# A two-block network in one kernel: VectorE makes the low weights of the up product from the ninth step on

## The chip, the core and the metric

The kernel runs on one core of one Trainium2 chip. The metric is device time in microseconds, the median of several executions. Engines: TensorE (PE; its weight loads are shown apart as PEld), VectorE (DVE), ScalarE (ACT), GpSimd (POOL) and SyncE (SP), which here issues nearly all transfers.

## What is computed

The reference is two blocks on 1024 tokens of width 1024 in float32, each with a feed-forward:

```
h = h + jnp.square(jax.nn.relu(m @ w_up[i])) @ w_down[i]         # first block,  m  = rmsnorm(h, norm_mlp[i])
x = x + jnp.square(jax.nn.relu(h2 @ w_up[l])) @ w_down[l]        # second block, h2 = rms_norm(x, norm_mlp_g[l])
```

with `w_up` 1024 x 4096 and `w_down` 4096 x 1024. Ahead of them stand attention and a gated delta rule (first block), or a pooling mixer and a gated recurrence (second block); the change leaves those alone but for the name of a semaphore at the start.

## The kernel before

**Split products.** A float32 product is made on TensorE from operands in a shorter format: each operand is a high part (rounded) plus a low part (value less high part), and high x high, high x low and low x high are added up. So every block of weights needs a high copy `w_hi`, made by ScalarE (`part_hi`, line 1735), and a low one `w_lo`, here made by GpSimd (`mlp`, lines 699 to 708) as four subtractions of 128 columns.

**The feed-forward** (`mlp` in each engine's program) uses a seven-product scheme for 2 x 2 blocks. The up product takes the 16 pairs of column blocks: pair 0 as two ordinary products, pairs 1 to 15 in seven steps each, 105 steps. The down product has four quarters `c` of seven products `q` with four column blocks `m`, 112 steps. A step is 12 matmuls of 128x512: eight with `w_hi` against the operand's high and low part, then, after a wait for `part_lo`, four with `w_lo`. Steps 105, the first of the down product, and 213 have the operand's low part last instead. The four slots of `w_hi` and `w_lo` rotate, so ScalarE makes the high weights of step g+4 when step g is over (`step_done`), GpSimd the low ones after that (`part_hi`), and `part_lo` counts the steps whose low weights are there.

**VectorE** makes the sums of weight blocks that are the sources of steps (`up_sum`, four per pair, into `w_raw` and `w_sum`), adds the products from PSUM into `tmp` (`up_step`), takes ReLU and scale (`relu_r`), forms the operand sums of the down product (`h_sums`, `h_last_sum`), and at the start the sums for operands 7, 5, 6 and 4 (`t_sums`, `t_lo`). In the down product it adds products (`down_step`), makes weight sums (`down_sums`, `down_sum4`), the low parts of the operands (`h_lo`) and, in the last quarter, the shared adds (`shared_adds`). Each engine works its list in order; a wait holds everything behind it.

**SyncE** loads blocks of `w_up` (`load_up`, line 544), stores operand sums to `h_ops` (`store`, line 560) and loads them back with `w_down` (lines 547, 557), also in the order written.

## Time and profile before

| | us |
|---|---|
| median of 3 runs | 2366.03 (2365.56 to 2367.23) |
| profiled execution | 2365.18 |
| its span, first to last instruction | 2363.4 |

| engine | busy us | share of the span | instructions |
|---|---|---|---|
| TensorE | 2339.2 | 99% | 15442 |
| VectorE | 1730.1 | 73% | 2319 |
| GpSimd | 1690.3 | 72% | 2442 |
| ScalarE | 924.0 | 39% | 1478 |

The granted TensorE clock is 0.998 of full speed over the span. The first feed-forward's 217 steps run from 553 to about 1147 us, the second's from 1753 to about 2350 us. Busy time of TensorE counts a matmul from its start to its modelled end, and matmuls overlap, so 99% does not say that none was late: that is read from the distance of their starts, or from how many of them a stretch holds.

### The profile page before, as it was taken

How to read it: one execution, taken by the hardware profiler on the slowest of the kernel's cores; microseconds unless marked ns; L12 is line 12 of the kernel's file. 1: busy time of each engine (PE TensorE's matmuls, PEld its weight loads, DVE VectorE, ACT ScalarE, POOL GpSimd, SP SyncE). 2: the span in 40 equal slices, each digit the busy share in tenths (PEclk: the TensorE clock that was granted, in tenths of full speed). 3: DMA queues.
4: the chain of work that ended last, by engine and by line, in shares of the span. 5: the costliest groups of instructions: out<-in, count | busy, mean ns of one | idle time of the engine just before them, and what ended most of it. 6: DMA issues, size and time to landing. Idle time of an engine off the chain costs nothing.

```text
span 2363.4 us, 40498 instructions
## 1 busy us (share of the span) xinstructions
PE 2339.2 (99%) x15442; PEld 1872.8 (79%) x15442; DVE 1730.1 (73%) x2319; ACT 924.0 (39%) x1478; POOL 1690.3 (72%) x2442
## 2 busy tenths in 40 slices
PE   9999999999999999999999999999999999999998
PEld 7767777777888888888788888888878888888886
DVE  4585656549777787789656777778388777888877
ACT  3152323225333343444424444444163333344443
POOL 5623444457988888988677766557669988898886
PEclk9999999999999999999999999999999999999999
DMA  5200000312444475443022111113114444654342
GB/s 173 72 19 29 29 28 28 117 36 89 166 153 150 147 252 194 170 152 116 19 80 92 46 37 37 37 44 119 47 48 174 156 148 147 241 194 150 125 144 106
DMA packets 110871, 254.55 MB, mean 108 GB/s; under 512 B 9440, under 2 KB 9952, under 8 KB 108512
## 3 DMA queue, kind: packets, MB, share of 16 engines
q1 hardware_dynamic: 105264, 233.43, 28.5%
q10 hardware_dynamic: 5424, 18.62, 2.3%
q8 instruction: 123, 2.02, 0.3%
q14 instruction: 60, 0.49, 0.1%
HBM read 181.75 MB, written 67.63 MB: 106 GB/s over the span
## 4 chain that ended last, share of the span: by engine, by line
PE 85%; DVE 7%; POOL 5%; DMA 1%; issue 1%; ACT 1%; SPq 0%; ACTq 0%; DVEq 0%; POOLq 0%
PE pairs L727 55%; PE mid L727 29%; POOL w_lo L707 4%; DVE work_r L2065 1%; DVE x_lo L2069 1%; DVE work L2486 1%; DVE work L2065 1%; DVE res L2065 1%; PE mid L847 1%; DMA x_lo_raw<-w_down 0%; DVE x_lo L2065 0%; DVE tmp L2065 0%; DVE res L2464 0%; DMA res<-x_t 0%; DMA work<-w_down 0%
## 5 line engine op out<-in xcount | busy, mean ns | idle before, releaser
L727 PE MATMUL pairs<-x_hi,w_hi 128*128 128x512 f32 x1576 | 533.7, 403 | 2.0 <-DVE x_lo L2069 0.9
L727 PE MATMUL pairs<-x_lo,w_hi 128*128 128x512 f32 x1576 | 519.5, 394 | 0.0
L727 PE MATMUL pairs<-x_hi,w_lo 128*128 128x512 f32 x1576 | 472.4, 393 | 0.4
L707 POOL TENSOR_TENSOR w_lo<-w_raw,w_hi 128x128 fp32r<-128x128 f32 x600 | 385.0, 675 | 55.3 <-ACT w_hi L1515 55.2
L673 POOL TENSOR_TENSOR idle<-idle 128x1 f32<-128x1 f32 x77 | 22.6, 293 | 483.9 <-PE pairs L727 474.3
L707 POOL TENSOR_TENSOR w_lo<-work,w_hi 128x128 fp32r<-128x128 f32 x512 | 314.9, 649 | 66.8 <-ACT w_hi L1515 64.9
L727 PEld LDWEIGHTS pairs<-x_hi,w_lo 128*128 128x128 f32 x1576 | 292.0, 188 | 65.3 <-POOL w_lo L707 3.8
L727 PEld LDWEIGHTS pairs<-x_hi,w_hi 128*128 128x128 f32 x1576 | 281.8, 188 | 76.9 <-issue 19.1
L727 PEld LDWEIGHTS pairs<-x_lo,w_hi 128*128 128x128 f32 x1576 | 291.8, 188 | 62.2 <-issue 2.1
L680 POOL TENSOR_TENSOR w_lo<-w_raw,w_hi 128x256 fp32r<-128x256 f32 x308 | 311.1, 1040 | 6.4
L676 POOL TENSOR_SCALAR w_hi<-w_raw 128x256 fp32r<-128x256 f32 x308 | 300.3, 999 | 0.0
L727 PE MATMUL pairs<-work_r,w_hi 128*128 128x512 f32 x1040 | 258.1, 390 | 0.0
L727 PE MATMUL mid<-work_r,w_hi 128*128 128x512 f32 x992 | 245.3, 389 | 0.0
L727 PEld LDWEIGHTS pairs<-work_r,w_hi 128*128 128x128 f32 x1040 | 194.9, 188 | 41.8 <-issue 1.4
L727 PEld LDWEIGHTS mid<-work_r,w_hi 128*128 128x128 f32 x992 | 186.1, 188 | 39.0
L2065 DVE TENSOR_TENSOR work<-work 128x512 f32<-128x512 f32 (+4 forms) x186 | 173.0, 944 | 27.0 <-DMA work<-res 15.1
L1515 ACT ACTIVATE w_hi<-work 128x512 fp32r<-128x512 f32 x128 | 80.6, 631 | 232.0 <-DVE work L2065 82.4
L1515 ACT ACTIVATE w_hi<-w_raw 128x512 fp32r<-128x512 f32 (+1 forms) x152 | 96.3, 635 | 184.9 <-DVE w_raw L2065 64.7
L707 POOL TENSOR_TENSOR w_lo<-x_lo_raw,w_hi 128x128 fp32r<-128x128 f32 x256 | 152.2, 630 | 8.5 <-ACT w_hi L1515 8.4
L707 POOL TENSOR_TENSOR w_lo<-w_sum,w_hi 128x128 fp32r<-128x128 f32 x240 | 133.0, 585 | 21.2 <-ACT w_hi L1515 21.2
L727 PE MATMUL mid<-x_hi,w_hi 128*128 128x512 f32 x376 | 146.4, 389 | 0.1
L727 PE MATMUL mid<-x_lo,w_hi 128*128 128x512 f32 x376 | 146.3, 389 | 0.0
(236 smaller groups left out, 3861.7 us busy)
## 6 DMA issues: line engine op xcount, KB each, us to landing
h_ops<-work SPq DMA_DIRECT2D x224, 256.0 KB, 3.8
w_raw<-w_stream SPq DMA_DIRECT2D x80, 512.0 KB, 3.5
w_raw<-w_up SPq DMA_DIRECT2D x120, 256.0 KB, 3.1
out_sq<-h_ops SPq DMA_DIRECT2D x28, 1024.0 KB, 5.1
x_lo_raw<-h_ops SPq DMA_DIRECT2D x28, 1024.0 KB, 5.5
work<-w_down SPq DMA_DIRECT2D x16, 1024.0 KB, 5.0
out_sq<-w_down SPq DMA_DIRECT2D x8, 1024.0 KB, 5.6
x_lo_raw<-w_down SPq DMA_DIRECT2D x8, 1024.0 KB, 5.3
```

The lines of the kernel that those rows point to most:

```text
L673: nc.gpsimd.tensor_tensor(idle[:, 0:1], idle[:, 1:2], idle[:, 1:2], ALU.add)
L676: ins = nc.gpsimd.tensor_scalar(w_hi[:, slot, part], w_raw[:, slot, part], 1.0, None, ALU.mult)
L680: ins = nc.gpsimd.tensor_tensor(w_lo[:, slot, part], w_raw[:, slot, part], w_hi[:, slot, part], ALU.subtract)
L707: ins = nc.gpsimd.tensor_tensor(low[:, part], raw[:, part], high[:, part], ALU.subtract)
L727: return nc.tensor.matmul(out, w, x, start=start, stop=stop)
L847: ins = nc.tensor.transpose(dst[:, c * P:(c + 1) * P], src[:, c * P:(c + 1) * P], ident)
L1515: return nc.scalar.activation(out, in_, func, **kw).then_inc(sem_out, 1)
L2065: return nc.vector.tensor_tensor(out, a, b, op).then_inc(sem_out, 1)
L2069: nc.vector.scalar_tensor_tensor(x_lo[:, j, :], res[:, j, :], par[:, gain + j:gain + j + 1], x_hi[:, j, :], ALU.mult, ALU.subtract).then_i ...
L2486: nc.vector.scalar_tensor_tensor(out, src, g, less, ALU.mult, ALU.subtract).then_inc(s["t_sum"], 1)
```

## The change

In both feed-forwards `VECTOR_UP`, the steps 9 to 104 of the up product, get their low weights from VectorE, one subtraction of 512 columns each (`weight_low`), issued after the VectorE work of the step four before. GpSimd skips them; before step 105 it waits until all are made. Three steps of the down product, 117, 201 and 205 (`VECTOR_LOW`), go to VectorE too; there GpSimd waits for VectorE (`vector_low`), does an operation of one column and counts the step in `part_lo`. ScalarE makes the high weights of steps 0 and 1 before the copies of operand 5, and those of steps 2 to 6 before the copies of operand 4 (before: 0 and 1 after operand 5, and 5 and 6 after operand 4). SyncE loads the fourth block of the next pair after two of the stores instead of after five. The semaphore `zeros` is folded into `stat_set`.

```diff
+        VECTOR_UP = range(9, U_STEPS)
+        VECTOR_LOW = (step_index(0, 3, 0), step_index(DCH - 1, 3, 0), step_index(DCH - 1, 4, 0))
...
-                        store_rest(i - 1)
-                        store_last(i - 1)
+                        if i == 1:
+                            store_rest(0)
+                            store_last(0)
+                        else:
+                            store_rest(i - 1, (2, 7))
+                            sp.wait_ge(s["part_lo"], g + 7)
+                            load_up(i + 1, A22)
+                            store_rest(i - 1, (5, 6))
+                            store_last(i - 1)
...
-                    if 1 < i < NPAIR - 1:
-                        sp.wait_ge(s["part_lo"], g + 7)
-                        load_up(i + 1, A22)
...
                     pool.wait_ge(s["part_hi"], b * STEPS + g + 1)
+                    if g in VECTOR_UP:
+                        continue
+                    if g == VECTOR_UP.stop:
+                        pool.wait_ge(s["part_lo"], b * STEPS + g)
+                    if g in VECTOR_LOW:
+                        pool.wait_ge(s["vector_low"], b * len(VECTOR_LOW) + VECTOR_LOW.index(g) + 1)
+                        nc.gpsimd.tensor_tensor(idle[:, 0:1], idle[:, 1:2], idle[:, 1:2], ALU.add).then_inc(s["part_lo"], 1)
+                        continue
...
-                t_hi(5)
                 part_hi(0)
                 part_hi(1)
+                t_hi(5)
                 t_hi(6)
-                part_hi(2)
-                part_hi(3)
-                part_hi(4)
+                for g in range(2, 7):
+                    part_hi(g)
                 t_hi(4)
...
-                    for ahead in {0: (), U_STEPS + 2: (), U_STEPS + 3: (3, 4), U_STEPS + 5: (), U_STEPS + 6: (3, 4)}.get(g, (4,)):
+                    for ahead in {0: (), 1: (), 2: (), U_STEPS + 2: (), U_STEPS + 3: (3, 4), U_STEPS + 5: (), U_STEPS + 6: (3, 4)}.get(g, (4,)):
...
+                def weight_low(g, signal):
+                    dve.wait_ge(s["part_hi"], g0 + g + 1)
+                    tt(half_slot(w_lo, u0, g), weight_source(u0, g), half_slot(w_hi, u0, g), ALU.subtract, signal)
...
                     up_step(1 + g // 7, g % 7)
+                    if g + 4 in VECTOR_UP:
+                        if g + 4 == VECTOR_UP.start:
+                            dve.wait_ge(s["part_lo"], g0 + VECTOR_UP.start)
+                        weight_low(g + 4, s["part_lo"])
...
+                    if U_STEPS + d + 4 in VECTOR_LOW:
+                        weight_low(U_STEPS + d + 4, s["vector_low"])
```

## Rows read from the trace of the kernel before

**Rows 1.** The page: busy time, and the chain that ended last by engine.
```profile
PE 2339.2 (99%) x15442; PEld 1872.8 (79%) x15442; DVE 1730.1 (73%) x2319; ACT 924.0 (39%) x1478; POOL 1690.3 (72%) x2442
...
PE 85%; DVE 7%; POOL 5%; DMA 1%; issue 1%; ACT 1%; SPq 0%; ACTq 0%; DVEq 0%; POOLq 0%
```

**Rows 2.** Windows, TensorE alone: stretch, length, busy (xmatmuls), clock, DMA share, GB/s.
```profile
563.87:608.33 44.46, 43.19 (x181) 1.00 0.42 147
611.05:828.65 217.60, 217.60 (x961) 1.00 0.44 154
883.12:891.94 8.82, 8.72 (x37) 1.00 0.75 255
1112.26:1135.95 23.69, 23.16 (x97) 1.00 0.20 68
1764.31:1791.34 27.03, 26.22 (x109) 1.00 0.45 159
2310.86:2334.55 23.69, 23.16 (x97) 1.00 0.14 45
```

**Rows 3.** Windows, steady up product: length, then PE, PEld, DVE, ACT, POOL busy.
```profile
610.00:822.00 212.00, 212.00 (x937) 175.56 (x936) 162.27 (x218) 79.05 (x135) 190.47 (x319) 1.00 0.45 157
```

**Rows 4.** Timeline of TensorE: start, us, engine line op, out<-in, count, [idle before <-releaser].
```profile
553.00 0.39 PE L727 MATMUL mid<-x_hi,w_hi 128*128 128x512 f32 x1
...
580.57 1.20 PE L727 MATMUL mid<-work_r,w_lo 128*128 128x512 f32 x4 [0.18 <-POOL w_lo L707]
...
1112.27 1.98 PE L727 MATMUL pairs<-work_r,w_hi 128*128 128x512 f32 x8
1114.40 1.20 PE L727 MATMUL pairs<-work_r,w_lo 128*128 128x512 f32 x4 [0.15 <-POOL w_lo L707]
```

**Rows 5.** Timeline of GpSimd at the start of the first up product.
```profile
548.41 4.67 POOL L707 TENSOR_TENSOR w_lo<-w_raw,w_hi 128x128 fp32r<-128x128 f32 x4 [10.66 <-ACT w_hi L1515]
...
566.61 2.24 POOL L707 TENSOR_TENSOR w_lo<-w_sum,w_hi 128x128 fp32r<-128x128 f32 x4 [2.30 <-ACT w_hi L1515]
...
577.43 9.62 POOL L707 TENSOR_TENSOR w_lo<-w_raw,w_hi 128x128 fp32r<-128x128 f32 x12 [1.29 <-ACT w_hi L1515]
```

**Rows 6.** Timeline of ScalarE: the high weights of step 5.
```profile
565.91 0.62 ACT L1515 ACTIVATE w_hi<-w_sum 128x512 fp32r<-128x512 f32 x1
```

**Rows 7.** Timeline of VectorE: low parts of two operands, GpSimd idle in both.
```profile
541.41 2.48 DVE L2065 TENSOR_TENSOR work_r<-work,work_r 128x512 fp32r<-128x512 f32 x4
...
564.78 2.48 DVE L2065 TENSOR_TENSOR x_lo<-work,x_hi 128x512 fp32r<-128x512 f32 x4
```

**Rows 8.** Timelines of VectorE and of GpSimd, one pair of the steady up product.
```profile
739.10 2.73 DVE L2065 TENSOR_TENSOR tmp<-tmp,mid 128x512 f32<-128x512 f32 x4 [1.34 <-PE mid L727]
...
748.71 2.69 DVE L2065 TENSOR_TENSOR work<-work 128x512 f32<-128x512 f32 x3
751.32 0.94 DVE L2065 TENSOR_TENSOR w_sum<-w_raw 128x512 f32<-128x512 f32 x1
...
739.87 1.72 POOL L707 TENSOR_TENSOR w_lo<-w_raw,w_hi 128x128 fp32r<-128x128 f32 x4 [0.54 <-ACT w_hi L1515]
```

**Rows 9.** Timelines of VectorE and of GpSimd: around the moved steps 117, 201 and 205.
```profile
872.47 0.68 DVE L2065 TENSOR_TENSOR tmp<-tmp,mid 128x512 f32<-128x512 f32 x1
...
875.50 0.68 DVE L2065 TENSOR_TENSOR tmp<-tmp,mid 128x512 f32<-128x512 f32 x1
...
1101.76 0.68 DVE L2065 TENSOR_TENSOR tmp<-tmp,pairs 128x512 f32<-128x512 f32 x1
...
1113.95 0.68 DVE L2065 TENSOR_TENSOR tmp<-tmp,mid 128x512 f32<-128x512 f32 x1
...
1117.85 0.67 DVE L2065 TENSOR_TENSOR tmp<-tmp,mid 128x512 f32<-128x512 f32 x1
...
1102.12 12.23 POOL L707 TENSOR_TENSOR w_lo<-x_lo_raw,w_hi 128x128 fp32r<-128x128 f32 x16
```

**Rows 10.** Timeline of GpSimd from step 117 on (four steps).
```profile
872.83 12.16 POOL L707 TENSOR_TENSOR w_lo<-x_lo_raw,w_hi 128x128 fp32r<-128x128 f32 x16
```

**Rows 11.** The tile `idle`: operations of one column, ns min/median/max.
```profile
L673 POOL TENSOR_TENSOR idle<-idle x77: 189/193/1482, 10.5 to 1727.2; 128x1 f32<-128x1 f32 x77
```

More of the change, by code:

```diff
@@ L477, in build @@
         for name in (
-            "zeros", "masks_in", "stat_set", "rope_in", "rope_part", "roped", "v_tok_psum", "v_tok",
+            "masks_in", "stat_set", "vector_low", "rope_in", "rope_part", "roped", "v_tok_psum", "v_tok",
             "s_psum", "s_merge", "s_masked", "s_exp", "s_sums", "pt_tri",
@@ L983, in _ @@
             GATES_AND_SUMS = {1: ((2, 3), ()), 3: ((4, 5), (0, 1, 2, 3)), 5: ((6, 7), (4, 5)), 7: ((), (6, 7))}
-            pe.wait_ge(s["zeros"], 1)
+            pe.wait_ge(s["stat_set"], 1)
             for n in range(WARM + WARM_AFTER):
@@ L2075, in take @@
                 tt(dst, pairs[:, parity % 2, :], r_tok[:, :], ALU.mult, evacuated)
-            nc.vector.memset(r_tok[:, 0:P], 0.0).then_inc(s["zeros"], 1)
+            nc.vector.memset(r_tok[:, 0:P], 0.0).then_inc(s["stat_set"], 1)
             dve.wait_ge(params_in, 16)
             nc.vector.memset(stat[:, :], 0.0).then_inc(s["stat_set"], 1)
-            dve.wait_ge(s["stat_set"], 1)
+            dve.wait_ge(s["stat_set"], 2)
             nc.vector.tensor_scalar(LESS_SINK, par[:, P_SINK:P_SINK + QH], -1.0, None, ALU.mult).then_inc(s["stat_set"], 1)
@@ L2216, in _ @@
             dve.wait_ge(s["masks_in"], 16)
-            dve.wait_ge(s["stat_set"], 2)
+            dve.wait_ge(s["stat_set"], 3)
             merge(0)
```

## Prediction

> **What bounds the kernel now.** I read the page first: TensorE is busy for 99% of the span, and the chain that ended last runs 85% on TensorE, 7% on VectorE and 5% on GpSimd [rows 1]. So the change can only win or lose what TensorE does not already fill. I number the 217 steps of one feed-forward 0 to 216 (0 to 104 are the up product, 105 to 216 the down product). A step is 12 matmuls, eight that need only the high weights and then four (its low part) that need the low ones. The windows say what a step costs when nobody is waited for: steps 20 to 99 are 960 matmuls in 217.60 us, 0.2267 us each, 2.72 us a step (a window also counts the one matmul that began before it, hence 961) [rows 2]. In the same way:
> - steps 4 to 18 of the first feed-forward: 44.46 us less 180 x 0.2267 = **3.66 us lost**;
> - steps 120 to 122 (first quarter of the down product): 8.82 - 8.16 = **0.66 us**;
> - steps 204 to 211 (last quarter): 23.69 - 21.76 = **1.93 us**;
> - second feed-forward, steps 4 to 12: 27.03 - 24.48 = **2.55 us**, and steps 204 to 211 again **1.93 us** [rows 2].
>
> That is 10.7 us, 0.45% of the time, and all that a faster supply of low weights can bring. GpSimd is busy for 190 of 212 us in the steady up product and VectorE for 162 [rows 3], but TensorE loses nothing there: that is two engines close to their limit, with no cost yet.
>
> **Who is late in the lossy stretches.** The low part of step 9 starts at 580.57, after idle time that GpSimd's `w_lo` (line 707) ended, and that of step 204 at 1114.40 in the same way [rows 4]. In steps 4 to 18 GpSimd starts its first low weights at 548.41, is starved after step 4, gets step 5's at 566.61, and from 577.43 works through steps 9 to 11 without a pause in 9.62 us, 3.2 us a step where TensorE takes 2.72 [rows 5]. Step 5's high weights themselves came late, at 565.91 [rows 6].
>
> **What an operation costs** (pitch: time from one start to the next, a group's time less the last one's own, over the others). VectorE with both inputs in SBUF: 4 in 2.48 us while GpSimd is idle, (2.48-0.68)/3 = 0.60 [rows 7]; beside GpSimd 3 in 2.69, (2.69-0.94)/2 = 0.87 [rows 8]. VectorE with a PSUM input: 4 in 2.73, 0.68, GpSimd active or not. A GpSimd piece (128 columns, four a step) beside those: (1.72-0.46)/3 = 0.42, so 1.7 us a step; beside two-input work it alternates with VectorE at 0.87, so 3.5 [rows 8].
>
> The Trainium skill ("SBUF — State Buffer", section on the two separate sides) says that the shared port pair is an exclusive lock: whoever starts first holds it for its whole instruction and the other fully blocks. Taken literally a piece and an operation would need 0.42 + 0.60 = 1.02 per pair, not the 0.87 of the rows; a quiet GpSimd would then give VectorE 0.42 per operation back, not 0.27, and each wait at the two moved steps at the end would be 0.6 us shorter. I go by the rows.
>
> **The change, part by part.**
>
> *Steady up product.* 96 steps in each feed-forward lose 4 GpSimd pieces and gain one VectorE subtraction of 512 columns. The trace has no such operation on VectorE; its bounds are 0.60 (alone) and 0.87 (contended) [rows 7, 8], and I take 0.60, since GpSimd then issues nothing. Per seven steps (19.04 us) VectorE has 12 two-input operations, 7 PSUM adds and now 7 low weights: 19 x 0.60 + 7 x 0.68 = 16.2 us, 85%. In-order waits: the low weight of step g+4 waits for ScalarE's copy, which waits for the end of step g, so VectorE is done with it about 1.4 us after that; in its worst step (four adds and a ReLU first, 3.3 us) after 4 us. TensorE wants it 10 us after. Behind the waiting VectorE stand only its own adds, whose banks have eight steps. The load of the next pair's weights moves up in SyncE's queue, ahead of three stores that have a pair's time. **0 us**, hidden by TensorE; if the cover were gone, see rival 3.
>
> *Start of the up product.* ScalarE makes the first high weights before the copies for operand 5, and those of steps 5 and 6 before operand 4. The early pieces cost VectorE 0.27 each as before, only sooner. I followed the queues from 543 us with the pitches above. ScalarE has step 5's high weights by 560 instead of 566.5, GpSimd makes step 4's low ones by 564.1, step 5's by 567.6 (wanted 568.4) and step 6's by 571.1 (wanted 571.1): the losses at steps 4 to 7, 0.9 us, shrink to about 0.1. GpSimd ends step 8 at 574.9. VectorE, which ends operand 4's lows at 568.4 (567.26 now [rows 7]), then has: weight sum 0.9, three differences 2.6, three adds and a ReLU of pair 1 with the fourth add 3.5, sum 0.6, add, ReLU, sum 1.9, add, ReLU, difference 1.9, and only then step 9's low weights, done at 580.4. TensorE, no longer delayed, wants them at 553.00 + 9 x 2.72 + 1.81 = 579.3 (step 0 starts at 553.00, [rows 4]; 1.81 is eight matmuls): **1.2 us lost** with the 0.1 of a restart (four matmuls after a wait take 1.20, [rows 4], where 3 x 0.2267 + 0.39 is 1.07), where 0.47 was. From there VectorE is ahead: step 10 at 582.3 (wanted 583.3), step 11 at 585.4 (586.0), step 16 at 598.3 (599.6), since SyncE now loads the fourth block before the stores. New loss 1.4 against 3.66 and 2.55: **-2.3 and -1.1 us**. Ends: a loss of 0.5 to 2.2 in each, so -5.2 to -1.8 together.
>
> *Step 117.* VectorE gets to it after the eight earlier steps of its own, GpSimd is free at 872.8 and now waits. VectorE, alone, does its four operations from 872.47 and the new one by 875.5, which is when it starts the next add today [rows 9, 10]; GpSimd passes the step with an operation of one column (0.19 median, [rows 11]) and starts step 118 at 875.8; today it starts it a quarter into its 12.16 us from 872.83 on, at 875.87. **0 us**, between -0.66 and +0.5.
>
> *Steps 201 and 205.* The same, and here it is what matters. VectorE runs behind: step 197 was over at 1095.95 (six steps of 2.72 before step 204's start at 1112.27, [rows 2, 4]), and its add comes at 1101.76 [rows 9]. So GpSimd, ready for step 201 at 1102.1, waits until VectorE has done its queue and the new operation (4 x 0.60, then it: 1105.4) and starts step 202 at 1105.7; today it makes 16 pieces from 1102.12 on in 12.23 [rows 9], and comes to step 202 at 1105.15. Nothing is gained for GpSimd; VectorE is 0.3 ahead. For step 205 GpSimd is ready at 1114.4 (1102.12 + 12.23), VectorE is done at 1117.5: its add of step 201, at 1113.95 today [rows 9], comes at 1113.65, then two lows, two sums and the new operation (today GpSimd needs 3.06 us from 1114.35: 1117.4). Adding the waits: 0.2 at 203, 0.3 at 204, 0.65 at 205, 0.4 at 208, 0.3 each at 209 and 210, 2.2 us against 1.93: **+0.3 us in each feed-forward**, +0.6. Ends: the whole 1.93 gone in both (-3.9), or a further us in each (+2.5).
>
> Sum: -2.3 - 1.1 + 0 + 0.6 = **-2.8 us**. On the profiled execution (2363.4 span, 2365.18 with what lies around it) 2362.4; the median of the runs is 0.85 above that, so 2366.03 - 2.8 = **2363.2 us**. Own range 2361 to 2365.5.
>
> **Rivals.**
> 1. *The last quarter is relieved after all.* If VectorE in GpSimd's waits runs further ahead than I reckon (by the lock of the skill, or because its lag is smaller), steps 202 on start a whole step earlier, and 1.93 goes twice: -3.4 - 3.9 = -7.3, **2358.7**. For: GpSimd has two steps of some 3 us less to make. Against: VectorE's lag of 5.8 us.
> 2. *The work is late on VectorE instead.* The start is set by VectorE's order, and steps 9 to 11 are as late by its queue as by GpSimd's: ramps -0.9 us twice, end +1 twice: about 0, **2366**. For: step 9 already is, in my replay.
> 3. *VectorE overflows in the up product* (the slower side). If its two-input operations stay at 0.87 without GpSimd, seven steps cost 19 x 0.87 + 7 x 0.68 = 21.3 us against 19.04, 2.3 us lost per pair of column blocks, 14 pairs twice: +63 us, **2429**. It decides from a mean pitch of 0.73 over the 26 operations on. Against: 0.60 at 541 us, where only GpSimd is missing [rows 7]. A small form of it, a wait for weights that land 3.8 us after the sum while 0.7 us is left, costs some 5 us, 2371.
>
> **How the numbers follow.** Forecast 0.50, rival 1 0.23, rival 2 0.17, rival 3 in its two forms 0.10. 0.2%, 4.7 us, is about what a measurement tells from no change. Faster by more: rival 1 and the lower tail of the forecast, 0.29. Slower by more: rival 3, 0.10. Same: 0.61. The range takes in rivals 1 and 2 and leaves rival 3 out: 2357.5 to 2367.5.
>
> **What would show it.** Right: no loss in steps 4 to 7, a wait at step 9's low part released by VectorE, none at 16 and 17; VectorE's two-input operations at 0.68 each and VectorE some 85% busy in the up product, GpSimd idle there; waits at steps 203 to 210 as before, GpSimd waiting for VectorE at 201 and 205. Wrong: step 204 on without waits (rival 1), or gaps at regular distances of seven steps (rival 3).

## The result and the profile after

| | before | after |
|---|---|---|
| median of 7 runs each, us | 2365.37 (2362.55 to 2367.23) | 2370.93 (2366.20 to 2376.44) |
| ratio, 95% interval | | 1.0023 [1.0014, 1.0032] |
| profiled execution, us | 2365.18 | 2376.44 (span 2374.6) |

The change makes the kernel 5.6 us slower, outside the range of the prediction (2357.5 to 2367.5) and next to the 2371 of the small form of rival 3. The runs of after also spread over 10 us where those of before spread over 5, and the profiled one is the slowest of its seven, so its rows show the loss at its largest: its span is 11.2 us longer than that of before, twice the difference of the medians.

The page of after, its first lines and its chain (beside [rows 1]):

```profile
PE 2345.6 (99%) x15442; PEld 1875.6 (79%) x15442; DVE 1786.8 (75%) x2517; ACT 921.0 (39%) x1478; POOL 1210.6 (51%) x1656
...
PE 76%; DVE 15%; DMA 4%; issue 3%; POOL 1%; ACT 1%; SPq 0%; ACTq 0%; DVEq 0%; POOLq 0%
PE pairs L741 51%; PE mid L741 24%; DVE tmp L2078 4%; DMA w_raw<-w_up 3%; DVE w_lo L2078 2%; DVE work L2078 2%; DVE x_lo L2082 1%; DVE w_raw L2078 1%; POOL w_lo L721 1%; DVE tmp L2532 1%; DVE res L2078 1%; DVE work L2499 1%; DVE w_sum L2078 1%; DVE work_r L2078 1%; PE mid L861 1%
```

GpSimd fell from 72% to 51% and left the chain (5% to 1%). VectorE doubled its share of it, and a transfer that carries weights of the up product, `w_raw<-w_up`, is on it with 3%. TensorE gave up 9 points.

Where the time went is read from windows of TensorE whose ends are the starts of steps. The length less 2.72 us a step is what the stretch lost. First feed-forward of after, steps 0 to 8, 9 to 19, 20 to 103, 104 to 107 and 108 to 130, then of the second steps 9 to 19 and 104 to 107 (columns as in [rows 2]):

```profile
552.84:577.80 24.96, 24.94 (x110) 1.00 0.31 106
577.80:609.26 31.46, 30.53 (x134) 1.00 0.46 156
609.26:838.19 228.93, 228.93 (x1010) 1.00 0.47 160
838.19:854.59 16.40, 13.57 (x49) 0.90 0.96 362
854.59:917.15 62.56, 62.56 (x277) 1.00 0.55 195
...
1782.20:1814.63 32.43, 30.83 (x133) 1.00 0.46 148
...
2043.88:2060.15 16.27, 13.56 (x49) 0.90 0.98 369
```

The same in before, steps 104 to 107 of the first feed-forward:

```profile
839.54:850.49 10.95, 10.95 (x50) 1.00 1.03 402
```

The table has all stretches, us lost in the first / in the second feed-forward:

| steps | before | after |
|---|---|---|
| 0 to 8 | 0.93 / 0.97 | 0.48 / 0.49 |
| 9 to 19 | 2.73 / 1.59 | 1.54 / 2.51 |
| 20 to 103 | 0.00 / 0.00 | 0.45 / 0.77 |
| 104 to 107, handover to the down product | 0.07 / 0.00 | **5.53 / 5.39** |
| 108 to 130 | 0.67 / 0.00 | 0.00 / 0.00 |
| 197 to 212 | 1.93 / 1.93 | 2.30 / 2.30 |

The sum of the two feed-forwards is 11 us worse in this execution, and 10.9 of it sits in four steps that the prediction never looked at. At the start the gain came in one feed-forward and not in the other.

### The profile page after: what moved, and what is told of

Same layout as the page of the kernel before. It is cut to its first block, busy times and chain, and to the rows that moved or that the text cites. A ratio compares the mean times of both kernels' runs of the same rounds, so it can differ in the third digit from the quotient of the medians.

```text
span 2374.6 us, 40016 instructions
## 1 busy us (share of the span) xinstructions
PE 2345.6 (99%) x15442; PEld 1875.6 (79%) x15442; DVE 1786.8 (75%) x2517; ACT 921.0 (39%) x1478; POOL 1210.6 (51%) x1656
## 4 chain that ended last, share of the span: by engine, by line
PE 76%; DVE 15%; DMA 4%; issue 3%; POOL 1%; ACT 1%; SPq 0%; ACTq 0%; DVEq 0%; POOLq 0%
PE pairs L741 51%; PE mid L741 24%; DVE tmp L2078 4%; DMA w_raw<-w_up 3%; DVE w_lo L2078 2%; DVE work L2078 2%; DVE x_lo L2082 1%; DVE w_raw L2078 1%; POOL w_lo L721 1%; DVE tmp L2532 1%; DVE res L2078 1%; DVE work L2499 1%; DVE w_sum L2078 1%; DVE work_r L2078 1%; PE mid L861 1%
## 5 line engine op out<-in xcount | busy, mean ns | idle before, releaser
L741 PEld LDWEIGHTS pairs<-x_hi,w_hi 128*128 128x128 f32 x1576 | 281.9, 188 | 75.4 <-issue 18.6
L2078 DVE TENSOR_TENSOR work<-work 128x512 f32<-128x512 f32 (+4 forms) x186 | 146.9, 805 | 27.8 <-DMA work<-res 15.5
L721 POOL TENSOR_TENSOR w_lo<-x_lo_raw,w_hi 128x128 fp32r<-128x128 f32 x240 | 139.2, 615 | 10.6 <-ACT w_hi L1529 10.4
L741 PE MATMUL pairs<-work_r,w_lo 128*128 128x512 f32 x520 | 139.9, 390 | 0.0
L741 PE MATMUL mid<-work_r,w_lo 128*128 128x512 f32 x496 | 134.9, 394 | 1.6 <-DVE w_lo L2078 1.6
```

The source lines that it names most:

```text
L721: ins = nc.gpsimd.tensor_tensor(low[:, part], raw[:, part], high[:, part], ALU.subtract)
L741: return nc.tensor.matmul(out, w, x, start=start, stop=stop)
L2078: return nc.vector.tensor_tensor(out, a, b, op).then_inc(sem_out, 1)
```

## Two places in the profile of after

**A loop with no slack.** I asked for the groups of VectorE in the steady up product, 611 to 828 us. The last column is the idle time before the group's operations and what ended it:

```profile
L2078 DVE TENSOR_TENSOR w_lo<-w_raw,w_hi 128x512 fp32r<-128x512 f32 x57 | 39.1, 686 | 0.0
...
L2078 DVE TENSOR_TENSOR w_sum<-w_raw 128x512 f32<-128x512 f32 x22 | 15.2, 689 | 27.7 <-DMA w_raw<-w_up 27.7
```

In that window VectorE is busy for 185.65 of 217.00 us, 85.6%, as forecast, and idle for 31.35. Of the idle time 27.7 us stand before one group, the weight sums into `w_sum`, and all of those were ended by one thing, the landing of the next block. One pair of it in time, VectorE and SyncE:

```profile
741.43 0.69 DVE L2078 TENSOR_TENSOR w_sum<-w_raw 128x512 f32<-128x512 f32 x1 [2.65 <-DMA w_raw<-w_up]
...
753.47 2.09 DVE L2078 TENSOR_TENSOR work<-work 128x512 f32<-128x512 f32 x3
755.47 0.69 DVE L2078 TENSOR_TENSOR w_sum<-w_raw 128x512 f32<-128x512 f32 x1
...
760.49 0.69 DVE L2078 TENSOR_TENSOR w_sum<-w_raw 128x512 f32<-128x512 f32 x1 [2.53 <-DMA w_raw<-w_up]
...
756.23 1.28 SPq L546 DMA_DIRECT2D w_raw<-w_up  x3
```

The first weight sum (`up_sum(i, 0)`) starts at 741.43 as its blocks land. VectorE works 22 operations without a pause to the fourth (`up_sum(i, 3)`, 755.47), 14.04 us later. That sum frees the buffer, SyncE issues the loads of A21, A11 and A12 at 756.23, and the next first sum starts at 760.49 when A21 and A11 are there, 5.02 us after the fourth. That is a closed loop of 14.04 + 5.02 = 19.06 us, and TensorE's pair takes 19.04. VectorE is idle in it for 2.5 us a pair and still cannot catch up: the idle time is the landing.

I measure VectorE's **lateness** as the time from the end of the fourth step of a pair (TensorE starts the next) to VectorE's first add for it. At 0.2 VectorE waits for TensorE. First / second feed-forward:

| pair | 3 | 4 | 6 | 8 | 10 | 14 |
|---|---|---|---|---|---|---|
| before | 3.60 / 3.24 | 2.20 / 2.84 | 0.45 / 0.50 | 0.20 / 0.20 | 0.20 / 0.20 | 0.20 / 0.20 |
| after | 5.57 / 5.15 | 5.49 / 5.16 | 5.08 / 5.87 | 5.18 / 5.52 | 5.55 / 5.37 | 6.13 / 5.68 |

Before, the way round while VectorE recovers is 12.48 + 5.2 us = 17.7, so it gains 1.4 us a pair on TensorE and the delay of the start is gone by the eighth pair. (Those 5.2 us mostly end with GpSimd's low weights and not with the landing; see the part on the prediction.) After, the lateness stays for the whole up product.

**The handover.** VectorE, SyncE and ScalarE of after at the last pair, whose first step (98) starts at 821.59:

```profile
830.39 2.09 DVE L2078 TENSOR_TENSOR work<-work 128x512 f32<-128x512 f32 x3
...
830.68 0.80 SPq L562 DMA_DIRECT2D h_ops<-work  x2
831.52 0.46 SPq L549 DMA_DIRECT2D work<-w_down  x1
832.33 2.30 SPq L562 DMA_DIRECT2D h_ops<-work  x3
...
840.92 0.63 ACT L1529 ACTIVATE w_hi<-work 128x512 fp32r<-128x512 f32 x1 [6.13 <-DMA work<-w_down]
```

And TensorE, where step 105 ought to run:

```profile
841.65 0.97 PE L741 MATMUL mid<-work_r,w_hi 128*128 128x512 f32 x2 [0.58 <-issue]
843.68 0.51 PE L741 MATMUL mid<-work_r,w_hi 128*128 128x512 f32 x1 [1.06 <-ACT work_r L1529]
845.37 0.50 PE L741 MATMUL mid<-work_r,w_hi 128*128 128x512 f32 x1 [1.18 <-ACT work_r L1529]
```

The same in before, where step 98 starts at 823.22:

```profile
827.80 0.80 SPq L560 DMA_DIRECT2D h_ops<-work  x2
831.57 0.33 SPq L547 DMA_DIRECT2D work<-w_down  x1
...
838.01 0.63 ACT L1515 ACTIVATE w_hi<-work 128x512 fp32r<-128x512 f32 x1 [5.22 <-DMA work<-w_down]
```

The late VectorE comes to the three `h_sums` 8.8 us after step 98 begins, not 1.7. SyncE's two stores wait for them, and the load of the first `w_down` block stands behind those stores. It starts 9.9 us into the step where it was 8.35, with two stores issued just ahead of it and three behind, and 9.4 us pass from its issue to ScalarE's first use. Before, the two stores were 3.8 us ahead, and 6.4 passed. ScalarE's copies stand in order behind that wait; TensorE waits for them. Of the 4.5 us by which the first use comes later in the step, 1.6 are the later issue and 3.0 the longer landing. The longer landing alone is enough: in the first handover of experiment 7 the load is issued 8.37 us into step 98, as early as in before, but behind two stores issued 0.84 and 0.42 us ahead of it. It takes 9.31 us, and 4.2 us are lost:

```profile
840.13 0.63 ACT L1529 ACTIVATE w_hi<-work 128x512 fp32r<-128x512 f32 x1 [6.07 <-DMA work<-w_down]
```

The last part is the clock. Windows of TensorE in the handover of after, 2 us each from 842 on:

```profile
842.00:844.00 2.00, 0.93 (x3) 1.00 1.02 396
844.00:846.00 2.00, 0.82 (x4) 1.00 0.68 255
846.00:848.00 2.00, 2.00 (x7) 0.53 0.75 209
848.00:850.00 2.00, 2.00 (x7) 0.61 1.05 404
850.00:852.00 2.00, 2.00 (x10) 1.00 1.05 408
```

After 4 us in which TensorE was busy for 1.75, the granted clock falls to the lower of its two levels (0.53 and 0.61 are means of a stretch with 1.2 GHz and one with 2.4) for some 3.5 us. That costs 2 x 0.47 + 2 x 0.39 = 1.7 of the 5.5 us.

## The experiments

All are timed in five rounds beside the kernel before on the same chip; their medians are compared with the 2365 to 2366 that before had beside them, and with the 2370.93 of after, which was timed once. Losses are given as first / second feed-forward; those at the handover are of steps 104 to 107. Each is read from one traced execution.

**1. Stop before the last pair.** GpSimd makes the last seven steps again.

```diff
-        VECTOR_UP = range(9, U_STEPS)
+        VECTOR_UP = range(9, U_STEPS - 7)
```

> The changed kernel, but VectorE stops at step 97 and GpSimd makes the low weights of the last seven steps of the up product (98 to 104) again. Theory H (handover): the changed kernel loses 5.4 to 5.5 us at steps 104 to 106 of each feed-forward, because VectorE's longer queue in the last pair delays the operand sums, and with them SyncE's stores and the load of the first block of the down product that stands behind them. With those seven operations gone most of that is back: 7 to 10 us less than the changed kernel, 2 to 4 us under the kernel before. Rival S (steady): the waits of single steps all over the up product (a low weight behind VectorE's adds) make the time; then at most 2 us come back and the kernel stays 3 to 4 us above the one before. Rival D (down): the moved steps 117, 201, 205 make it; then nothing comes back.

Measured: 2368.67 (2364.80 to 2373.32), ratio 1.0016 [1.0007, 1.0025]. The handover loses 0.01 / 0.00 us instead of 5.53 / 5.39, the `h_sums` come 3.4 and 5.2 us into step 98. The window of the first handover:

```profile
839.18:850.07 10.89, 10.89 (x50) 1.00 1.03 399
```

2.3 of the 5.6 us are back with seven steps of 96, where I had expected 7 to 10. The rest isn't, and the spread remains: the time is still 3.3 us above that of before, as rival S said, though the traced execution pays nothing at the handover. It loses 1.3 us more than before in the other stretches of the two feed-forwards; where the slower executions lose time is open. VectorE is still late at pair 14 (2.8 / 4.6 us).

**2. None of the three steps in the down product.**

```diff
-        VECTOR_LOW = (step_index(0, 3, 0), step_index(DCH - 1, 3, 0), step_index(DCH - 1, 4, 0))
+        VECTOR_LOW = ()
```

> The changed kernel with GpSimd making the low weights of steps 117, 201 and 205 again. Theory H: those three steps are worth 0 to 0.5 us each way: the loss in steps 203 to 210 is 2.3 us in each feed-forward with the move and was 1.93 without, and the 0.66 us at steps 120 and 121 of the first comes back or not; so within 1 us of the changed kernel, some 5 us above the one before. Rival D (down): the move costs, and without it the time falls by 3 us or more.

Measured: 2370.28 (2364.67 to 2375.90), ratio 1.0017 [1.0007, 1.0027], the time of after. Steps 197 to 212 lose 1.89 / 1.90, not 2.30: the three moved steps cost 0.4 us in each feed-forward. The two handovers of this one execution differ. In the first the `h_sums` come 6.0 us into step 98 and nothing is lost, in the second 7.6 us, and 4.3 are.

**3. The load of `w_down` ahead of the stores in the last pair.**

```diff
-                        store_rest(i - 1, (2, 7))
                         sp.wait_ge(s["step_done"], g + 3)
                         load_down(0, A11)
+                        store_rest(i - 1, (2, 7))
```

> The changed kernel, but in the last pair SyncE waits for step 100 and loads the first block of the down weights before it stores operand sums 2 and 7 of pair 14, instead of after. Theory H in its strict form (the load is late because it stands behind stores that wait for VectorE): it is issued 1.2 us sooner relative to TensorE, lands before the four stores' traffic, and 4 to 9 us of the 11 of both handovers come back, the kernel is at or a few us under the one before. Rival Q (VectorE's and ScalarE's own queues are late in the handover, the load is not what holds them): under 2 us come back.

Measured: 2368.89 (2366.96 to 2373.00), ratio 1.0013 [1.0005, 1.0022]. The handovers lose nothing with the `h_sums` 6.3 and 5.9 us into step 98. SyncE and ScalarE in it:

```profile
832.36 0.34 SPq L549 DMA_DIRECT2D work<-w_down  x1
832.75 3.02 SPq L562 DMA_DIRECT2D h_ops<-work  x5
...
838.46 0.63 ACT L1529 ACTIVATE w_hi<-work 128x512 fp32r<-128x512 f32 x1 [3.73 <-DMA work<-w_down]
```

6.1 us from issue to use, with the stores behind. But 6.3 and 5.9 lie on the harmless side in experiment 2 too, so this execution does not separate the order from the lateness. The median is 2.0 us below that of after, and 4 to 9 had been expected. The trace shows that lateness is paid in other places too: outside the handovers the two feed-forwards lose 2.9 us more than in before, 1.5 of them at steps 34 and 35 of the first, behind one landing of 6.86 us instead of some 5.

**4. The kernel before with only ScalarE's new order** (`t_hi(5)` after `part_hi(1)`, `part_hi(2)` to `part_hi(6)` ahead of `t_hi(4)`).

> The kernel before with only ScalarE's new order at the start of each up product (high weights of steps 0 and 1 ahead of operand 5, those of 5 and 6 ahead of operand 4). All low weights by GpSimd. Theory: the losses at steps 4 to 7 (0.9 us in each feed-forward) shrink to about 0.4, those at 9 to 17 stay, so 0.5 to 1.5 us in all under the kernel before, hardly to be told from none. Rival O (order): the early high weights make VectorE late at the start, 1 us or more above it.

Measured: 2366.19 (2364.08 to 2368.10), ratio 1.0002 [0.9994, 1.0011]. Steps 0 to 8 lose 0.50 / 0.53 where before lost 0.93 / 0.97, steps 9 to 19 lose 2.27 / 2.29. The early high weights save 0.4 us at steps 4 to 7, half of the 0.8 that the prediction counted there, and nothing clear behind.

**5. The fourth sum first.** One swap on VectorE, no operation more or less: the fourth weight sum no longer stands behind the three `h_sums`.

```diff
                         if i > 1:
-                            h_sums(i - 1)
                             up_sum(i, 3)
+                            h_sums(i - 1)
```

> The changed kernel with one swap in VectorE's list: at the first step of a pair the fourth weight sum comes ahead of the three operand differences instead of after them. The operations are the same. Theory L (loop): in the changed kernel the chain first weight sum, VectorE's list of 14.0 us, fourth weight sum, load of the next pair's blocks (5.0 us), next first weight sum is 19.04 us long, exactly what TensorE takes for a pair, so VectorE never gets back the 5 to 6 us it is late after the first pairs. The swap takes 1.8 us out of the loop: the lateness of its adds at the fourth step of a pair falls from 5-6 us to under 1 us by the sixth pair, the waits of TensorE in steps 20 to 103 and at the handover (104 to 107) go, and the time is 4 to 7 us under the changed kernel's. Rival B (busy): VectorE is late because it has too much to do (26 operations a pair); then the swap changes nothing in the lateness.

Measured: **2365.22** (2362.66 to 2365.67), ratio 0.9994 [0.9984, 1.0003]. The list from first to fourth sum is 12.03 us instead of 14.04, the lateness is 2.36 at the third pair and 0.20 from the fourth on, and the handover loses nothing. VectorE's group of weight sums, 611 to 828 us, and the window of the first handover:

```profile
L2078 DVE TENSOR_TENSOR w_sum<-w_raw 128x512 f32<-128x512 f32 x23 | 15.8, 688 | 2.8 <-DMA w_raw<-w_up 1.5
```

```profile
837.09:847.97 10.88, 10.88 (x49) 1.00 1.03 402
```

The 27.7 us of waiting for the landing are 1.5. The same work on the same engine, 5.7 us faster: the amount of work was not the cause, its place was. The swap changes two things, though. It takes 2.0 us out of the list, and the low weights that the load of A12 waits for now stand behind the `h_sums`, so that load is issued 2.18 us behind A11's and not 0.48. Experiment 10 shortens the list alone, experiment 13 moves the load alone.

**6. The same swap, and none of the three steps of the down product** (experiments 2 and 5 together).

> The swap of the other kernel, and the steps 117, 201 and 205 back on GpSimd. Theory L: within 1 us of the swap alone (1.9 instead of 2.3 us lost at 197 to 212, but 0.7 more or less at 108 to 130), the lateness again under 1 us. Rival D (down): 2 us or more apart from it.

Measured: 2363.77 (2361.04 to 2365.36), ratio 0.9990 [0.9981, 0.9999]. It is the only version whose interval lies below that of the kernel before, by 0.1%, which is less than what I called measurable. It is 1.45 us below experiment 5, where 1 at most had been expected; the spreads of the two overlap, and steps 197 to 212 account for 0.8 of it.

**7. Another order inside the loop.** The low weights of the step ahead are made before the four adds of the fourth step, not behind them.

```diff
+                    early = g % 7 == 3 and g + 4 in VECTOR_UP and g + 4 > VECTOR_UP.start
+                    if early:
+                        weight_low(g + 4, s["part_lo"])
                     up_step(1 + g // 7, g % 7)
...
-                    if g + 4 in VECTOR_UP:
+                    if g + 4 in VECTOR_UP and not early:
```

> The changed kernel, but at the fourth step of each pair VectorE makes the low weights ahead of its four adds and ReLU instead of behind them. Theory L: the loop is as long as before, so VectorE stays 5 to 6 us late and the handover still costs up to 5 us in some feed-forwards; but the low weights of a pair's first step come 3.2 us sooner, so the waits at steps 14, 35, 49, 91 and the like, 0.5 to 1.5 us in each feed-forward, go. 1 to 3 us under the changed kernel. Rival B: the adds are what is short of time; 0 or slower.

Measured: 2370.95 (2368.12 to 2373.08), ratio 1.0019 [1.0010, 1.0028]. From pair 3 on the low weights of the first step of each pair are ready 2.3 to 4.7 us before TensorE wants them; in after it was 1.2 us at most, and up to 0.9 too late. Yet nothing is gained where 1 to 3 us had been expected. The waits move one step on, to the second step of a pair (0.90 us at step 36 of the first feed-forward, 0.58, 0.50 and 0.41 at steps 15, 85 and 92 of the second), and steps 20 to 103 lose 1.0 / 1.0 us. The loop is as long as in after, and the handovers lose 4.2 / 2.9 us, with the `h_sums` at 7.2 and 8.8. It is the lateness that costs, whichever low weights come first behind it.

**8. Only the start.** VectorE makes steps 9 to 20, GpSimd everything else.

```diff
-        VECTOR_UP = range(9, U_STEPS)
+        VECTOR_UP = range(9, 21)
```

> VectorE makes the low weights of steps 9 to 20 alone, GpSimd all later ones and those of 117, 201 and 205. Theory L: VectorE is rid of the extra work before the loop matters, catches up in some pairs as in the kernel before, no waits in steps 30 to 103 and none at the handover; the start loses what the changed kernel's does (0.5 and 1.5 to 2.5 us). Within 1.5 us of the kernel before, on either side. Rival R (start): the start itself is what costs in the changed kernel; then 3 us or more above the one before.

(`VECTOR_LOW` is empty here too.) Measured: 2366.21 (2361.95 to 2369.65), ratio 1.0002 [0.9993, 1.0011]. Steps 0 to 19 lose 1.9 / 2.4 us against 3.7 / 2.6 in before. What the start can give is 2 us at most and does not show in the time.

**9. The swap in the kernel before.** The diff of experiment 5 on the kernel in which GpSimd makes the low weights.

> The kernel before, with one swap: the fourth weight sum ahead of the three h differences at the first step of each pair. In the kernel before, GpSimd makes the low weights, VectorE's way round from the first weight sum of a pair to the next takes some 17.9 us of the 19.04 that TensorE takes for a pair (its lateness falls by 1.3 us a pair), and the handover to the down product loses nothing. Theory of the loop: the swap only speeds up a recovery that is complete anyway; lateness is gone two pairs earlier, steps 9 to 107 lose as before, the time is that of the kernel before within 1.5 us (ratio 0.9995 to 1.0005). Rival, that the swap is a gain of its own with any maker of the low weights: 5 us or more below before, ratio 0.998.

Measured: 2365.29 (2362.27 to 2368.16), ratio 0.9997 [0.9988, 1.0006]. The swap is worth nothing there. It is no gain of its own; it repairs what the change did.

**10. One step of seven back to GpSimd** (the first of each pair, from step 14 on).

```diff
-        VECTOR_UP = range(9, U_STEPS)
+        VECTOR_UP = [g for g in range(9, U_STEPS) if g < 14 or g % 7]
...
-                    if g == VECTOR_UP.stop:
+                    if g == U_STEPS or 14 <= g < U_STEPS:
                         pool.wait_ge(s["part_lo"], b * STEPS + g)
...
-                        if g + 4 == VECTOR_UP.start:
+                        if g + 4 == 9 or g + 4 > 14 and (g + 4) % 7 == 1:
```

> The changed kernel, but from step 14 on GpSimd makes the low weights of one step in seven (the first of each pair), as in the kernel before; six of seven stay with VectorE. Theory of the loop: the list of VectorE from the first to the fourth weight sum shrinks from 14.04 to 13.44 us, the way round from 19.04 to about 18.4, so its lateness falls by 0.6 us a pair, from 5.5 us at the third pair to 0.2 near the twelfth; the three h differences of the last handover come some 3 us after the start of step 98 instead of 8.5, steps 104 to 107 lose under 0.5 us instead of 5.4 in each feed-forward: 2365 us (2363.5 to 2367). Rival, that the loss grows with the work on VectorE (one seventh undone, one seventh of the loss back): 2370. The dead point that the loop is not closed by this list but by something else: lateness still 5 us at pair 14.

Measured: 2364.44 (2362.74 to 2366.81), ratio 0.9995 [0.9986, 1.0004]. A seventh of the move undone takes all of the loss back. A12's load stays 0.48 us behind A11's and the landing stays at 5.1 us in the middle; the list alone is shorter, 13.44 us, lateness in the first feed-forward goes 5.75, 5.64, 5.06, 3.65, 2.66, 0.20 (pairs as in the table above), in the second it is still 1.80 at pair 14, and the handovers lose nothing. VectorE in it, fourth sum and next first sum:

```profile
738.74 0.69 DVE L2078 TENSOR_TENSOR w_sum<-w_raw 128x512 f32<-128x512 f32 x1 [1.91 <-DMA w_raw<-w_up]
...
752.17 0.69 DVE L2078 TENSOR_TENSOR w_sum<-w_raw 128x512 f32<-128x512 f32 x1
...
757.62 0.69 DVE L2078 TENSOR_TENSOR w_sum<-w_raw 128x512 f32<-128x512 f32 x1 [2.96 <-DMA w_raw<-w_up]
```

**11 and 12. One operation more a pair, inside or outside the loop.** VectorE makes one low weight twice in 12 pairs of each feed-forward. In experiment 11 it is at the sixth step of a pair (shown), between the first and the fourth sum. In experiment 12 it is at the first (`g % 7 == 0`), behind the fourth sum.

```diff
                     if g + 4 in VECTOR_UP:
+                        if 14 <= g < 98 and g % 7 == 5:
+                            weight_low(g + 4, s["vector_low"])
+                            dve.wait_ge(s["vector_low"], 15 * b + g // 7 - 1)
```

> The changed kernel, with one low weight made twice by VectorE in each of twelve pairs, at the sixth step, between the first and the fourth weight sum (one operation of 0.60 us and a wait for itself, 0.72 together). Theory of the loop: the way round goes from 19.04 to 19.76 us, 0.72 lost a pair, 12 pairs in each of two feed-forwards less the half to one us of slack in each: 15 to 17 us more than the changed kernel, some 2386. Rival, busy time: VectorE then has 16.9 us of work in 19.04, and nothing is lost: 2371. Rival, only the spread of the landings is lost: 1 to 3 us more, 2373.

> The same extra operation and the same number of them as in the run beside this one, but at the first step of a pair, behind the fourth weight sum, where VectorE waits some 2.5 us for the load of the next weights to land. Theory of the loop: the wait gets 0.72 us shorter and nothing else moves: 2371, the time of the changed kernel within 1.5 us. Rival, busy time or contention of VectorE as a whole: the same time as with the operation inside, whatever that is.

Measured inside: **2389.21** (2385.70 to 2390.45), ratio 1.0099 [1.0084, 1.0115], from four executions, 18.3 us more than after for 24 operations of 0.72 us (15 to 17 expected). Steps 20 to 103 now lose 6.0 / 10.3 us. The list is 14.76:

```profile
724.19 0.69 DVE L2078 TENSOR_TENSOR w_sum<-w_raw 128x512 f32<-128x512 f32 x1 [2.23 <-DMA w_raw<-w_up]
...
738.96 0.69 DVE L2078 TENSOR_TENSOR w_sum<-w_raw 128x512 f32<-128x512 f32 x1
...
744.48 0.69 DVE L2078 TENSOR_TENSOR w_sum<-w_raw 128x512 f32<-128x512 f32 x1 [3.03 <-DMA w_raw<-w_up]
```

Measured outside: **2366.36** (2362.34 to 2368.31), ratio 0.9998 [0.9989, 1.0007]. Here I was wrong: I had expected the 2371 of after. The same operation as in experiment 11, as often, and the kernel is 4.6 us *faster* than without it, 22.9 us faster than with it inside the loop. The rows say where:

```profile
734.91 0.68 DVE L2078 TENSOR_TENSOR w_sum<-w_raw 128x512 f32<-128x512 f32 x1
...
738.92 0.69 DVE L2078 TENSOR_TENSOR w_sum<-w_raw 128x512 f32<-128x512 f32 x1 [0.79 <-DMA w_raw<-w_up]
...
735.67 1.61 SPq L546 DMA_DIRECT2D w_raw<-w_up  x3
```

The landing takes 4.01 us where it took 5.02. The three loads are spread over 1.61 us instead of 1.28, since A12's waits for the low weights that the extra operation delays: it is issued 0.90 us behind A11's and not 0.48. Most pairs of the run show the same (4.0 to 4.4, a few 4.9 to 6.0). The next two runs separate this from the operation.

**13. A12 later, nothing else.**

```diff
-                        sp.wait_ge(s["part_lo"], g + 5)
+                        sp.wait_ge(s["part_lo"], g + 5 + (i > 1))
                         load_up(i + 1, A12)
```

> The changed kernel, with one wait on SyncE one step later: the load of the pair's third block (A12) waits for the low weights of the next step, so it starts some 1.2 us after the load ahead of it (A11) instead of 0.48; no operation is added or moved on another engine, and the two stores behind the load move along. In the run with the extra operation outside the loop this distance was 0.90 us and the first weight sum came 4.1 to 4.2 us after the fourth instead of 5.05. Theory of the shared queues (a load that starts right behind slows the one ahead): the first weight sum comes 4.0 us after the fourth, the way round is 18.1 us, the lateness falls by 0.9 us a pair, steps 104 to 107 lose nothing: 2365.5 us (2363.5 to 2367). Rival, the extra operation itself did it: the way round stays 19.1 us and the time 2371.

Measured: **2364.88** (2361.39 to 2368.57), ratio 0.9998 [0.9989, 1.0007]. VectorE's fourth and next first sum, and SyncE's loads:

```profile
748.67 0.69 DVE L2078 TENSOR_TENSOR w_sum<-w_raw 128x512 f32<-128x512 f32 x1
...
752.71 0.69 DVE L2078 TENSOR_TENSOR w_sum<-w_raw 128x512 f32<-128x512 f32 x1 [1.55 <-DMA w_raw<-w_up]
...
749.43 2.09 SPq L546 DMA_DIRECT2D w_raw<-w_up  x3
```

A landing of 4.04 us (4.0 to 4.3 in nearly all pairs), 14.04 + 4.15 = 18.2 us round, lateness in the first feed-forward 4.55, 3.75, 2.10, 2.55, 1.32, 0.20, and no loss at either handover. One wait moved by one step on an engine that computes nothing brings the 6 us back.

**14. The stores later.** A12 stays where it is, the two stores behind it (operands 2 and 7) go behind A22.

```diff
-                            store_rest(i - 1, (2, 7))
                             sp.wait_ge(s["part_lo"], g + 7)
                             load_up(i + 1, A22)
+                            store_rest(i - 1, (2, 7))
                             store_rest(i - 1, (5, 6))
```

> The changed kernel, with the two stores (operands 2 and 7) behind the load of the fourth block (A22) instead of ahead of it; the load of A12 stays 0.48 us behind that of A11. If it is the stores behind A12 that slow the load of A11, the first weight sum comes some 4.1 us after the fourth and the time is 2366. If it is A12's own traffic, it stays at 5.0 us and the time is 2370 to 2372, with the handover 0.5 to 1 us later because the stores are.

Measured: 2364.78 (2364.18 to 2367.97), ratio 1.0002 [0.9992, 1.0011]. The landing is 4.1 to 4.7 us (once 5.3), 4.5 in the middle. Neither branch of the expectation fits alone, and both causes count: the stores so close behind cost some 0.5 us of the landing (5.05 to 4.50 in the middle), and A12's load, moved off together with them in experiment 13, another 0.3 (to 4.17). Either change alone leaves the loop enough slack, since 0.5 us a pair over 12 pairs is the 5 to 6 us of lateness.

## Why the prediction was wrong

**The step that failed is "Steady up product ... 0 us, hidden by TensorE".** Its terms for VectorE's own work were right. The operations are 0.69 long and 0.60 apart, and it is 85.6% busy where 85% was forecast. What failed is that the busy share decides nothing here. VectorE and SyncE's loads form a loop, and the loop is full at 85% busy. The text came near it once, in the last sentence of rival 3: weights that land 3.8 us after the sum, 0.7 us left, some 5 us lost, 2371. That is the time measured, and the cause in outline. It had a share of the 0.10 given to rival 3.

**The term that was mis-sized is the landing.** The small form of rival 3 took the 3.8 us between the end of the fourth sum and the next first sum, 4.77 from start to start, as the time that the weights need. Before, it mostly isn't that. The first sum also waits for low weights of GpSimd, and of the idle time before this group in before, 611 to 828 us, they end the greater part:

```profile
L2065 DVE TENSOR_TENSOR w_sum<-w_raw 128x512 f32<-128x512 f32 x23 | 20.0, 869 | 35.2 <-POOL w_lo L707 24.6 <-DMA w_raw<-w_up 10.6
```

In 20 of the 26 pairs that I read in the two feed-forwards, the blocks lay ready when GpSimd released the sum. The second of them, A11, landed 2.93 us after its issue (the median), which is 4.3 us after the start of the fourth sum. In after it lands 3.90 us after its issue and 5.03 after that sum, although the sum itself became 0.25 us shorter. The text let the load of A22 move ahead of three stores and took SyncE's queue as harmless ("ahead of three stores that have a pair's time"). It did not see that A12's load, which used to wait for GpSimd, would now follow A11's at 0.48 us where it had followed at 1.61. In before the three issues span 2.30 us (this pair is one of the six that a landing ended):

```profile
752.34 2.30 SPq L544 DMA_DIRECT2D w_raw<-w_up  x3
...
756.09 0.69 DVE L2065 TENSOR_TENSOR w_sum<-w_raw 128x512 f32<-128x512 f32 x1 [2.96 <-DMA w_raw<-w_up]
```

A faster producer released a transfer earlier, and that slowed the transfer ahead of it. In experiment 13, with A12's load 1.38 us behind, A11 lands 3.01 us after its issue again, the loop has 0.8 us of slack, and the step of the prediction holds: 0 us.

**The place of the loss was not in the text at all.** It expected gaps at distances of seven steps if the loop filled up. They came, but small (0.45 and 0.77 us in 84 steps, at steps 35, 49, 91 and 98). In this execution nearly all of the lateness was paid at the handover, where three in-order lists hang on it one behind the other: VectorE's sums, SyncE's stores ahead of the load, ScalarE's copies. With the `h_sums` below some 7 us into step 98 it is free: at 6.0, 6.3, 5.9 and 5.2 nothing was lost. Above, 7.2, 7.6, 8.3, 8.8, 8.8, 9.1 and 9.6 lost 4.2, 4.3, 5.4, 2.9, 5.5, 1.8 and 4.4. Two things order the scatter. One is when the `w_down` load lands: in the handovers that lose under 0.1 us it does so 15.0 us into step 98 at the latest; at 15.02 and 15.12 (experiments 4 and 8) 0.25 and 0.35 us are lost; in these seven it lands at 17.7, 18.0, 18.9, 18.0, 19.3, 16.4 and 18.6. Six of the seven loads take 8.0 to 9.4 us behind two stores issued just ahead, where without them it is 5.1 to 6.8; the seventh, that of the loss of 1.8, takes 6.3 though it has the same stores ahead. The other is the clock: in the windows of the two small losses (2.9 in experiment 7, 1.8 in experiment 11) the granted clock is 1.00, in the five others 0.89 or 0.90. Why that one load was fast, and what makes the clock fall in one and not in the other, stays open. That two such handovers may or may not be lost in a run fits the 10 us between the fastest and the slowest run of after; but the other executions have no trace, and experiment 1 spreads over 8.5 us with handovers that lose nothing in its trace.

**The start.** Forecast: 0.1 us at steps 4 to 7, 1.2 at step 9, none at 10, 11 and 16. Measured in the first feed-forward: 0.46 (0.14 at step 5 and 0.32 at step 6), 1.08 and 0, with VectorE done with step 9's low weights at 580.5 (forecast 580.4). TensorE waits where the text said:

```profile
580.57 1.20 PE L741 MATMUL mid<-work_r,w_lo 128*128 128x512 f32 x4 [0.80 <-DVE w_lo L2078]
```

Missed was step 14 (0.43 / 1.10 us, and 0.28 at step 13 of the second): the low weights of a pair's first step are issued behind the four adds and the ReLU of the fourth step before, with VectorE still late. With it the gain of -2.3 and -1.1 became -1.6 and +0.4.

**Steps 117, 201 and 205.** +0.3 us was forecast in each feed-forward, 2.2 lost against 1.93; measured 2.30 against 1.93 here, and 1.9 without the three steps (experiments 2 and 6). GpSimd waits 3.44 us for VectorE at step 201 and starts 202 at 1109.17:

```profile
1109.03 0.19 POOL L716 TENSOR_TENSOR idle<-idle 128x1 f32<-128x1 f32 x1 [3.44 <-DVE w_lo L2078]
1109.17 8.73 POOL L721 TENSOR_TENSOR w_lo<-x_lo_raw,w_hi 128x128 fp32r<-128x128 f32 x12
```

Nothing is relieved, so rival 1 is out. At step 117 the forecast of 0 could not be judged in after, whose TensorE came there 5.5 us late; in experiment 5, with no such delay, steps 108 to 130 lose 0.79 / 0.63 against 0.67 / 0.00 in before. It is not the moved step that does it: in experiment 6, without it, they lose 0.85 / 0.71.

**Rival 3 in its large form** (two-input operations stay at 0.87, 2429) is out: they are 0.60 apart. Its point of decision, a mean pitch of 0.73, counted the work against the 19.04 us of a pair. Experiments 11 and 12 show which count is right: 0.72 us more inside the loop cost 18 us, and outside it nothing.

## What to carry to other kernels

Before work is moved to an engine that is "only 85% busy", look for the loop that runs through it: the list between the instruction that frees a buffer and the one that needs its refill, plus the landing, against the bottleneck's time for the same piece of work. Work between those two instructions costs its full price once they add up to the period; work behind the freeing instruction is free up to the landing, so put the instruction that frees the buffer as early in the list as its inputs allow. And a loss of slack is paid where the phases change: follow the lateness to the next handover, not only through the steady stretch.

## What the runs showed of the hardware

A late handover was paid for twice. In five of seven the granted clock fell to 1.2 GHz after the gaps at steps 104 and 105. In after the 12 matmuls from 847.04 to 850.97 took 3.93 us where 12 take 2.72 at 2.4 GHz (0.43 us from start to start at the lower level, 0.23 at the higher), and some 3.8 us of gaps so became a loss of 5.5.

In the loop a transfer was slowed by those issued close behind it on the same queue. The second block of 256 KB was used 5.05 us after the sum that frees its buffer (the median of 26 pairs) with a third load 0.48 us behind and two stores after it, 4.50 without the two stores, and 4.17 with the third load 1.38 us behind and the stores after that. The Trainium skill ("DMA: Bandwidth & Descriptors", section on queues, rings and completion order) says that on each DMA engine descriptors are consumed in ring order, while a later one may finish its write before an earlier one. The rows agree that transfers of one queue overlap; they show besides that being first in order does not keep a transfer's landing from being delayed. It is not so everywhere: the 1 MB load of `w_down` took 6.1 / 6.6 us in experiment 3 with five stores issued from 0.4 us behind it on, and 6.4 / 6.0 in before. There the stores just ahead count, with 9.4 / 9.4 us in after.

VectorE with GpSimd silent starts a two-input operation of 128x512 every 0.60 us over whole pairs, its own duration 0.69, as the four operations of [rows 7] had shown; a step's four pieces on GpSimd beside it cost VectorE's list less than the one operation that replaced them. The list from first to fourth sum was 12.48 us with GpSimd's pieces and 14.04 with five low weights in it, 1.56 us more for 3.0 us of work: the other 1.4 is what VectorE's other operations gained with GpSimd silent.
